# The memory projection of a layer: its operands made in the stage ahead, its banks copied by ScalarE, its post-norm and residual on VectorE

## The reference, cut to what matters

```python
y = mixer(u, ...)                                   # 512 x 1024
h = h + rms_norm(y, mix_post_g[i])                  # post-norm of the mixer
u = rms_norm(h, mem_pre_g[i])
y = memory_cross_attention(u, rms_norm(mem, mem_kv_g[i]), x_wq[i], x_wkv[i], x_wo[i])

def rms_norm(x, g):
    y = x * rsqrt(mean(x * x, axis=-1) + EPS)
    return y * g

def memory_cross_attention(u, mem_n, wq, wkv, wo):
    q = split_heads(u @ wq, 4)
    k, v = jnp.split(mem_n @ wkv, 2, axis=-1)       # 256 x 2048: the memory projection
    ...
```

## Time and profile before

| | us |
|---|---|
| median of 3 runs | 3198.81 (3192.93 to 3199.34) |
| the profiled execution | 3198.18 |
| its span in the trace | 3196.4 |
| TensorE busy | 3080.0 (96%) |
| VectorE busy | 1793.0 (56%) |
| ScalarE busy | 1253.3 (39%) |
| GpSimd busy | 343.2 (11%) |
| mean granted clock of TensorE | 0.978 |

### The profile page before, as it was taken

One profiled execution on the slowest core, in us unless ns is written; L12 is line 12 of the kernel. 1 busy time (PEld: TensorE's weight loads), 2 busy tenths in 40 slices (PEclk: granted clock), 3 DMA queues, 4 the chain that ended last, 5 costly groups with the idle time before them and its releaser, 6 DMA issues.

```text
span 3196.4 us, 37515 instructions
## 1 busy us (share of the span) xinstructions
PE 3080.0 (96%) x14826; PEld 2431.1 (76%) x14826; DVE 1793.0 (56%) x2558; ACT 1253.3 (39%) x1982; POOL 343.2 (11%) x252
## 2 busy tenths in 40 slices
PE   7999999999999999999998999999999989999998
PEld 5777888887767888886657877888766678778886
DVE  7766544367766544466665635443567656354444
ACT  6645322245554323344444433222334434332222
POOL 2011100011011000021002212000200022120001
PEclk9999999999999999999999999999999999999999
DMA  3111233232112232322112322333211123222332
GB/s 135 53 47 54 93 99 97 94 99 73 54 40 74 95 99 93 98 92 66 53 47 99 106 73 73 99 96 96 73 63 57 40 86 112 73 73 93 99 99 79
DMA packets 73722, 259.09 MB, mean 81 GB/s; under 512 B 8020, under 2 KB 10200, under 8 KB 73176
## 3 DMA queue, kind: packets, MB, share of 16 engines
q1 hardware_dynamic: 72824, 252.99, 24.4%
q0 software_dynamic: 736, 3.87, 0.3%
HBM read 254.73 MB, written 2.10 MB: 80 GB/s over the span
## 4 chain that ended last, share of the span: by engine, by line
PE 88%; DVE 7%; issue 2%; ACT 1%; DVEq 1%; DMA 0%; POOLq 0%; POOL 0%; ACTq 0%
PE bank L480 72%; PE bank L954 2%; PE bank L965 1%; DVE w_lo L1931 1%; PE bank L651 1%; PE bank L975 1%; PE bank L979 1%; PE bank L1150 1%; PE bank L1171 1%; PE bank L991 1%; PE bank L911 1%; PE bank L507 1%; PE bank L693 1%; DVE r_x L1966 1%; ACT w_hi L1273 1%
## 5 line engine op out<-in xcount | busy, mean ns | idle before, releaser
L480 PE MATMUL bank<-a_hi,w_hi 128*128 128x512 f32 x2168 | 879.7, 406 | 36.8 <-DVE w_lo L1931 15.2
L480 PE MATMUL bank<-a_hi,w_lo 128*128 128x512 f32 x2168 | 850.4, 392 | 0.0
L480 PE MATMUL bank<-a_lo,w_hi 128*128 128x512 f32 x2168 | 849.8, 392 | 0.0
L1931 DVE TENSOR_TENSOR w_lo<-w_raw,w_hi 128x1024 fp32r<-128x1024 f32 (+1 forms) x474 | 610.5, 1289 | 288.1 <-ACT w_hi L1273 286.8
L1273 ACT ACTIVATE w_hi<-w_raw 128x1024 fp32r<-128x1024 f32 (+1 forms) x474 | 495.6, 1046 | 440.5 <-DMA w_raw<-weights 440.5
L480 PE MATMUL bank<-b_hi,w_hi 128*128 128x512 f32 (+1 forms) x1560 | 594.6, 381 | 17.9 <-DVE w_lo L1931 10.7
L480 PE MATMUL bank<-b_lo,w_hi 128*128 128x512 f32 (+1 forms) x1560 | 583.9, 374 | 0.0
L480 PE MATMUL bank<-b_hi,w_lo 128*128 128x512 f32 (+1 forms) x1560 | 583.8, 374 | 0.0
L480 PEld LDWEIGHTS bank<-a_hi,w_hi 128*128 128x128 f32 x2168 | 411.2, 190 | 143.4 <-issue 40.2
L480 PEld LDWEIGHTS bank<-a_lo,w_hi 128*128 128x128 f32 x2168 | 411.7, 190 | 90.2 <-issue 8.6
L480 PEld LDWEIGHTS bank<-a_hi,w_lo 128*128 128x128 f32 x2168 | 410.4, 189 | 88.7
(11 more groups left out here) (295 smaller groups left out, 3003.9 us busy)
## 6 DMA issues: line engine op xcount, KB each, us to landing
w_raw<-weights SPq DMA_DIRECT2D x458, 512.0 KB, 3.5
w_raw<-weights SPq DMA_DIRECT2D x16, 384.0 KB, 3.0
x<-x SPq DMA_DIRECT2D x8, 256.0 KB, 7.4
mem<-mem POOLq DMA_DIRECT2D x2, 1024.0 KB, 5.2
out<-x SPq DMA_DIRECT2D x8, 256.0 KB, 2.1
mem<-mem SPq DMA_DIRECT2D x1, 1024.0 KB, 12.4
ple<-ple POOLq DMA_DIRECT2D x2, 512.0 KB, 4.0
o<-c_level SPq DMA_DIRECT2D x1, 512.0 KB
```

Of the source, the lines that this page charges most:

```text
L480: last = mm(bank[unit_bank(u) if at is None else at][:, 0:cols], w[:, u % SLOTS, ks], t[:, k, 0:cols], start=(k == begun and n == 0), stop ...
L1931: tt(w_lo[:, u % SLOTS, w], w_raw[:, u % SLOTS, w], f32(w_hi[:, u % SLOTS, w]), ALU.subtract).then_inc(w_lo_ready, 1)
```

## The change

In out2, VectorE multiplies the memory's tiles by r_mem (in place, two in each of the units k = 2 to 5), ScalarE and VectorE round two in each of the units 3 to 6, and VectorE, not ScalarE, waits for the memory's transfer. In kv, TensorE forms the sums of squares as token columns behind unit 0 and spreads the reciprocal root behind unit 1. ScalarE copies the 16 banks to kv_y (`kept`), ahead of its weight split in each step. VectorE scales y's tile k from the bank, drains, adds it to x's tile k itself, then splits weights up to unit 4+k, then makes a_lo of tile k-2. GpSimd's additions to x are gone. The whole diff:

```diff
--- before.py
+++ after.py
@@ -322,7 +322,7 @@
         ple_landed, mem_first_landed, mem_landed, dil_landed = sem("ple_landed"), sem("mem_first_landed"), sem("mem_landed"), sem("dil_landed")
         pos_first_landed, pos_landed = sem("pos_first_landed"), sem("pos_landed")
         p_hi_ready, p_ready, e_made, e_taken = sem("p_hi_ready"), sem("p_ready"), sem("e_made"), sem("e_taken")
-        y_scaled, x_finished = sem("y_scaled"), sem("x_finished")
+        y_scaled, x_finished, mem_normed = sem("y_scaled"), sem("x_finished"), sem("mem_normed")
         t_made, conv_made, g_qk, gates_split, gates_log, gates_made, g_end = (
             sem("t_made"), sem("conv_made"), sem("g_qk"), sem("gates_split"), sem("gates_log"), sem("gates_made"), sem("g_end"))
         g_cols, g_ends, g_copied, g_gate, g_valued, g_v, g_ones = (
@@ -1108,8 +1108,12 @@
             def kv(l):
                 h = operands(2, l)[1]
                 unit(h, cols=MEM, ready=h_ready)
-                sum_squares()
-                for _ in range(3):
+                pe.wait_ge(sq_added, c.count(sq_added, 8))
+                pe.wait_ge(root_ready, c.groups)
+                column_sums(SUM_BANK, sq_sum, True, True)
+                unit(h, cols=MEM)
+                spread_root(SUM_BANK)
+                for _ in range(2):
                     unit(h, cols=MEM)
                 with c.loop(3, {}, 4):
                     for _ in range(4):
@@ -1696,9 +1700,8 @@
                             square(y[:, k, :])
                         else:
                             f(y[:, 18, :], y[:, 7, :], ACT.Square).then_inc(y_squared, 1)
-                        if mixed and k == 4:
-                            act.wait_ge(mem_landed, 16 * (l + 1))
-                        for j in ((2 * k - 8, 2 * k - 7) if mixed and k >= 4 else ()):
+                        for j in ((2 * k - 6, 2 * k - 5) if mixed and 3 <= k < 7 else ()):
+                            act.wait_ge(mem_normed, 8 * l + j + 1)
                             f(b_op[0][:, j, 0:MEM], mem[:, j, :], ACT.Copy, scale=col("mem_kv", l, j)).then_inc(h_hi_ready, 1)
 
                     step(squares)
@@ -1803,12 +1806,20 @@
                 ahead(first + 3 * PAIRS + 3)
 
             def kv(l):
-                root_of_mean()
+                first = c.unit
+
+                def kept(u):
+                    act.wait_ge(unit_done, u + 1)
+                    if u == first:
+                        act.wait_ge(bank_free, first)
+                    f(kv_y[:, u - first, :], bank[unit_bank(u)][:, 0:MEM], ACT.Copy).then_inc(bank_free, 1)
+
+                root_of_columns(SUM_BANK)
                 for k in range(8):
-                    step()
+                    step(kept)
                     round_x(a_op, k, col("mem_pre", l, k), squared=False)
                 for k in range(8):
-                    step()
+                    step(kept)
                     square(x[:, k, :])
 
             def cross(l):
@@ -2408,7 +2419,11 @@
             def out2(l, mixed=False):
                 for k in range(8):
                     step(lambda u, b: dve.tensor_copy(y[:, k, :], b[:, :]).then_inc(bank_free, 1))
-                    for j in ((2 * k - 8, 2 * k - 7) if mixed and k >= 4 else ()):
+                    if mixed and k == 2:
+                        dve.wait_ge(mem_landed, 16 * (l + 1))
+                    for j in ((2 * k - 4, 2 * k - 3) if mixed and 2 <= k < 6 else ()):
+                        tt(mem[:, j, :], mem[:, j, :], r_mem[:, :], ALU.mult).then_inc(mem_normed, 1)
+                    for j in ((2 * k - 6, 2 * k - 5) if mixed and 3 <= k < 7 else ()):
                         dve.wait_ge(h_hi_ready, c.count(h_hi_ready))
                         stt(b_op[1][:, j, 0:MEM], mem[:, j, :], col("mem_kv", l, j), f32(b_op[0][:, j, 0:MEM]),
                             ALU.mult, ALU.subtract).then_inc(h_ready, 1)
@@ -2573,32 +2588,24 @@
                 ahead(first + 3 * PAIRS + 3)
 
             def kv(l):
-                def scaled(u, b):
-                    t = c.pick(u - first, 4)
-                    tt(kv_y[:, t, :], b[:, 0:MEM], r_mem[:, :], ALU.mult).then_inc(bank_free, 1)
-
                 first = c.unit
-                recip(r_post)
 
                 def post_scaled(k):
-                    stt(y[:, k, :], y[:, k, :], col("mix_post", l, k), r_post[:, :], ALU.mult, ALU.mult).then_inc(y_scaled, 1)
-
-                post_scaled(0)
-                post_scaled(1)
+                    stt(y[:, k, :], y[:, k, :], col("mix_post", l, k), bank[SUM_BANK][:, :], ALU.mult, ALU.mult)
+                    dve.drain()
+                    tt(x[:, k, :], x[:, k, :], y[:, k, :], ALU.add).then_inc(x_ready, 1)
+
+                recip_of_columns()
                 for k in range(8):
-                    dve.wait_ge(unit_done, c.unit + 1)
-                    scaled(c.unit, bank[unit_bank(c.unit)])
-                    if k + 2 < 8:
-                        post_scaled(k + 2)
-                    if c.next < c.unit + SLOTS:
-                        split_lo()
-                    c.unit += 1
-                    if k:
-                        lo_x(a_op, k - 1, col("mem_pre", l, k - 1))
-                lo_x(a_op, 7, col("mem_pre", l, 7))
-                with c.loop(2, {}, 4):
-                    for _ in range(4):
-                        step(scaled)
+                    post_scaled(k)
+                    ahead(first + SLOTS + k)
+                    if k >= 2:
+                        lo_x(a_op, k - 2, col("mem_pre", l, k - 2))
+                for k in (6, 7):
+                    lo_x(a_op, k, col("mem_pre", l, k))
+                ahead(first + 16 + SLOTS - 1)
+                dve.wait_ge(bank_free, first + 16)
+                c.unit += 16
 
             def cross(l):
                 first, heads = c.unit, C_HEADS * l
@@ -2771,8 +2778,6 @@
                 pool.wait_ge(f_taken, PAIRS * (l + 1))
                 pool.dma_start(mem[:, :, :], dram["mem"].rearrange("p (a b) -> p a b", a=DT)).then_inc(mem_landed, 16)
                 add_squares()
-
-                add_scaled()
                 add_squares()
 
             def xo(l):
```

## The result

| | before | after |
|---|---|---|
| median, us | 3197.68 (4 runs) | 3215.82 (3213.20 to 3220.85, 4 runs) |
| profiled execution, us | 3198.18 | 3215.49 |
| its span, us | 3196.4 | 3213.7 |

The ratio is 1.0061, 95% interval 1.0048 to 1.0073: the change makes the kernel slower, by 18.1 us in the medians. The direction was the one forecast (+8.3 us); the size was more than twice that, and 3215.82 lies just above the range's 3215.

What follows compares the result with a forecast made beforehand. TensorE was taken to bound the kernel, losing some 12 us a layer in the memory projection, VectorE's until unit eight. Ring +7.3 and clock +1.0 gave +8.3 us on 3198.18, 3206.5, plus 0.63 for the median: 3207 us, range 3196 to 3215.

Steps and rivals of the forecast that it cites:

- What bounds the kernel: Memory projection, stage kv: TensorE needs 46.9 us for 16 units, some 12 us a layer lost; VectorE's until unit eight.
- the ring: In kv, VectorE waits for w_hi behind ScalarE's rounding of its x tile: turns 4.60, then 5.26 us; chance 0.70.
- The rival without a ring: In kv, w_hi runs ahead of rounding, VectorE steps take 3.31 us, stage 48.8 us, time 3178 us; chance 0.13.
- Memory prepared ahead: In out2, two r_mem products a step, 0.7 us, fit VectorE's 2.45 us wait for w_hi; cost nothing.
- T: Start of the first memory unit in kv, 1729.3 us in layer 0; the forecast's times count from it.
- the spreading: In kv behind unit 1, TensorE's spreading of the reciprocal root was put at 0.89 us at full clock.
- VectorE's first tile: In kv, VectorE was to start its first tile at T+7.7, where the reciprocal ended at T+12.5 before.
- The 5.3 us a layer: In out2, the price named for the memory products if VectorE's wait gave no cover.
- The end of the ring: In kv, unit 11 ends T+50.7; three a_lo and w_lo of unit 12, 3.2 us, end T+51.0.
- The clock: In kv, TensorE's lower clock on the last unit behind a gap costs 0.5 us a layer, +1.0 in sum.
- The rival with the low clock: In kv, each 2.3 us gap lowers the clock: last unit costs 2.0 us a layer, 3210 us; chance 0.10.
- The sum: Stage kv ends near T+62.7 against 59.9 and 58.4 us: +2.9 and +4.4 us, +7.3 in sum.

Runs made afterwards that it cites:

- the kernel with the ring open: Changed kernel with VectorE splitting weights one unit less far: 3178.24 us; with out2's memory work also put before its weight split: 3176.87 us.
- three edits that open it: Changed kernel with VectorE's split one unit less far, ScalarE's w_hi before rounding x, or x tiles one ahead: 3178.24, 3177.11, 3179.74 us.
- one that lengthens it: Changed kernel with the additions to x given back to GpSimd: 3223.43 us, ratio 1.0083.
- the last experiment: Changed kernel with VectorE's split one unit less far and, in out2, its memory products and roundings before its weight split: 3176.87 us, ratio 0.9936.
- the two with weights first in the tail: Changed kernel with w_lo of unit 12, or of units 12 to 14, made ahead of the last two a_lo: 3209.14 and 3210.02 us.

## Why the prediction was right and wrong, point by point

**What bounds the kernel.** Right: the kernel with the ring open has the stage at 49.8 to 50.4 us, close to the 48.8 us that the rows gave for TensorE alone. The rival without a ring had said 3178 us for a kernel that was not the one changed; the runs without a ring gave 3177 to 3180, with stages 1.0 to 1.6 us longer than its 48.8.

**The ring.** Right in place, order and size: turns of 4.65 and 5.32 us against 4.60 and 5.26, shown by three edits that open it and one that lengthens it. The first rounding with a gain column takes 0.63 us from start to start, not the 0.54 that I took from an operation without one; the copy of 256 columns takes 0.27 us, not 0.30.

**Memory prepared ahead: "the two products of a step, 0.7 us, fit in there".** Wrong. VectorE's wait there is part of a round trip with ScalarE, and the products stand behind it, not in it. Cost: VectorE's copy 0.5 us late and TensorE 0.46 us idle before the sum, so unit 1 began at T+4.4, not T+3.9 (it begins at T+3.9 in the last experiment, where that wait is gone). The rest is the spreading, 1.05 us where I had 0.89, and 0.1 us in unit 1 and behind the spreading: VectorE's first tile began at T+8.5, not T+7.7. The 5.3 us a layer that I named as the price of a lost cover is in no sum, and it is wrong too: 8 products at 0.33 us are 2.6 us a layer.

**The end of the ring: "unit 11 runs to T+50.7; VectorE has three a_lo and w_lo of unit 12 to do, 3.2 us, T+51.0".** This is the term that failed. Unit 12 started at T+54.9. Of the 3.9 us, 1.4 are inherited (0.8 from the first tile, 0.4 from seven turns, 0.2 until unit 11 starts behind its w_lo), and 2.4 arise here (5.6 us from unit 11 to unit 12, where I had 3.2 and my own prices give 3.1), from two causes that cover each other: unit 11 took 4.6 us at the half clock, and a_lo and w_lo ran beside GpSimd's squares of x, which begin when ScalarE has rounded the last tile. I had costed a_lo at 0.66 us because "GpSimd is idle in these steps": true of the eight steps and not of what follows them. The stage came to 66.7 where I had 62.8 in both layers.

**The clock: 0.5 us a layer.** Too small: 1.5 us, in the three layers of these runs where the gap before unit 11 was 2.19 us long. That "the gap is shorter than any that lowered it" was true of the memory stage alone. Elsewhere the trace of before has gaps of this length, and behind them both levels, as these starts and the 3 us behind each show:

```profile
143.18 0.46 PE L651 MATMUL bank<-h_q,h_k 64*128 64x128 f32 x3 [2.37 <-DVE h_d L2131]
...
1677.96 0.47 PE L480 MATMUL bank<-a_hi,w_hi 128*128 128x512 f32 x1 [2.13 <-DVE a_lo L1976]
...
143.18:146.18 3.00, 3.00 (x31) 3.00 (x32) 3.00 (x5) 1.33 (x3) 0.00 (x0) 0.57 0.19 78
1677.96:1680.96 3.00, 3.00 (x14) 2.43 (x15) 2.62 (x6) 1.19 (x4) 0.00 (x0) 1.00 0.00 0
```

The rival with the low clock was right in kind, with 2.0 us where 1.5 came. The Trainium skill, "TensorE: Matmul & The Clock Gate", Part 1, has the lower rate as the default that activity lifts; the granted 0.68 in the units behind 2.19 us of idle time, beside 1.00 in those behind 0.69 us, agrees.

**The sum.** 62.8 became 66.7 in both layers, so +7.3 became +15.1 us; the clock's +1.0 is contained in that. Another 2.2 us of the profiled execution lie outside the stage, in the scatter of the other stages; without them the median would be near 3213.6 us, inside the range, with the same term wrong.

## What to carry to other kernels

Where two engines run in fixed order and each makes something that the other needs, write down what stands between one hand-over and the next on both; the longest closed round set the pace here, and how busy either engine was said nothing. Splitting weights *further* ahead closed the ring here: more lead for one product was less lead for the other, and one unit less took 38 us off. And when costing work as hidden, ask whether the idle time it is to fill is idle on the way to it or behind it.

## What was not expected of the hardware

TensorE's clock alternated from unit to unit under a steady rhythm: with 24 matmuls every 5.32 us it was granted 1.00 in one turn and 0.68 in the next, the gap before the unit being 0.69 us and 2.19 us in turn (the shorter gap follows because the slow unit lasts longer). It is not a fixed alternation. In the changed kernel and the two with weights first in the tail, 18 units of the ring start behind a gap of 2.18 to 2.20 us: 15 of them fell to the lower level on the way, and 3 ran at 1.00 to the end, each followed by a second such gap and a slow unit; the 12 behind 0.7 to 0.8 us all ran at 1.00. What decides it these runs leave open.

A ScalarE operation with a gain column takes 0.72 us where one without takes 0.62 us (128x512, both in kv; without a column also the a_hi of the earlier trace rows); GpSimd is idle beside the slower one, so contention with GpSimd is not the cause.

Beside GpSimd an a_lo took 1.77 us in place of 0.74, and GpSimd's addition 2.2 in place of 1.28. In the kernel before the addition that belongs to the earlier trace rows is

```profile
1760.43 2.20 POOL L2734 TENSOR_TENSOR x<-x,y 128x512 f32<-128x512 f32 x1 [1.62 <-DVE y L2584]
```

It starts inside the w_lo (1760.27 to 1761.48) and ends 1.15 us behind it, about an addition's length; the a_lo then ends 0.54 us behind the addition, about an a_lo's length from start to start. So the three look like a queue, each standing until the one ahead is done, and not like two that share.
